# Row sums of a spatial gating weight moved from TensorE to VectorE, with a new place for the offsets and a new VectorE order

## What is computed

```
h = rms_norm(x); u, v, q, k, v2 = split(h @ w_in)
# spatial unit, blocks of 128 rows, 4 groups h of 128 channels
v = layer_norm(gelu(v), ln_g, ln_b)                  # ln_g, ln_b: one value per channel
w = where(mask, sgu_w, 0)                            # [4, 128, 128], upper right 64x64 corner is zero
mixed[p, c] = sum_q w[h][p, q] * v[q, c] + sgu_b[h, p]
y_a = gelu(u) * mixed
```

## Time and profile before

| | |
|---|---|
| median of 3 runs | 916.4 us |
| the profiled execution's own time | 916.97 us |
| its span in the trace | 915.2 us |
| TensorE busy | 906.9 us (99%) |
| VectorE, ScalarE, GpSimd busy | 593.3, 427.7, 394.2 us |
| granted TensorE clock | 0.999 of full speed |

### The profile page before, as it was taken

How to read it: one execution, slowest core, us unless ns; L and a number is a source line. 1 busy time by engine, 2 the same in 40 slices (tenths; PEclk the granted TensorE clock), 3 DMA queues, 4 the chain that set the end, 5 groups by cost and what they waited for, 6 DMA issues and landing times.

```text
span 915.2 us, 11923 instructions
## 1 busy us (share of the span) xinstructions
PE 906.9 (99%) x4209; PEld 747.4 (82%) x4209; DVE 593.3 (65%) x783; ACT 427.7 (47%) x832; POOL 394.2 (43%) x388
## 2 busy tenths in 40 slices
PE   9999999999999999999999999999999999999997
PEld 7888887787878888888888888888888888888885
DVE  6548989986679777475364653646557676544754
ACT  6637548857556533243333333333335455444451
POOL 1449743331243478567485675755754000000021
PEclk9999999999999999999999999999999999999999
DMA  9798465221343272743726437264367996556543
GB/s 338 229 270 253 105 171 137 70 88 51 110 121 105 81 229 75 225 149 116 230 82 218 148 117 230 84 216 148 117 211 255 355 392 200 196 191 199 185 138 138
DMA packets 152363, 159.58 MB, mean 174 GB/s; under 512 B 27752, under 2 KB 109680, under 8 KB 152304
## 3 DMA queue, kind: packets, MB, share of 16 engines
q1 hardware_dynamic: 151472, 157.89, 53.6%
q10 hardware_dynamic: 832, 0.92, 0.4%
HBM read 117.78 MB, written 40.50 MB: 173 GB/s over the span
## 4 chain that ended last, share of the span: by engine, by line
PE 83%; DVE 5%; DMA 3%; SPq 3%; issue 3%; POOL 2%; ACT 1%; POOLq 0%; DVEq 0%; ACTq 0%
PE ps L862 27%; PE ps L864 26%; PE ps L863 26%; DMA xs<-in_x 1%; SPq L387 1%; PE ps L1017 1%; PE ps L1042 1%; DVE wB_lo L1837 1%; PE ps L1029 1%; PE ps L1111 1%; DVE D_lo L1843 1%; DMA hT_raw<-in_xT 1%; POOL s L726 1%; DVE wA_lo L1837 1%; POOL by_offset L671 1%
## 5 line engine op out<-in xcount | busy, mean ns | idle before, releaser
L2096 DVE TENSOR_TENSOR P_lo<-P_raw,P_hi 128x512 fp32r<-128x512 f32 x132 | 124.2, 956 | 82.4 <-ACT P_hi L1536 76.7
L862 PE MATMUL ps<-T_hi,P_hi 128*128 128x512 f32 x352 | 136.9, 389 | 0.0
L863 PE MATMUL ps<-T_lo,P_hi 128*128 128x512 f32 x352 | 136.9, 389 | 0.0
L864 PE MATMUL ps<-T_hi,P_lo 128*128 128x512 f32 x352 | 136.9, 389 | 0.0
L804 POOL TENSOR_TENSOR wd<-wd 128x256 f32<-128x256 f32 x88 | 81.6, 928 | 93.4 <-DMA wd<-in_w_down 88.2
L862 PE MATMUL ps<-rb_hi,ra_hi 128*128 128x512 f32 x308 | 119.8, 389 | 0.0
L863 PE MATMUL ps<-rb_lo,ra_hi 128*128 128x512 f32 x308 | 119.8, 389 | 0.0
L864 PE MATMUL ps<-rb_hi,ra_lo 128*128 128x512 f32 x308 | 119.8, 389 | 0.0
L1650 ACT ACTIVATE ra_hi<-ra 128x512 fp32r<-128x512 f32 x77 | 48.6, 631 | 98.5 <-DMA rb<-w_down_T 59.8
L649 POOL TENSOR_SCALAR late<-late 128x1 f32<-128x1 f32 x12 | 6.1, 506 | 189.7 <-ACT junk L1718 176.2
L2205 DVE TENSOR_TENSOR ra_lo<-ra,ra_hi 128x512 fp32r<-128x512 f32 x77 | 55.8, 725 | 37.4 <-ACT ra_hi L1650 37.1
(11 more groups left out here) (281 smaller groups left out, 2012.7 us busy)
## 6 DMA issues: line engine op xcount, KB each, us to landing
wd<-in_w_down SPq DMA_DIRECT2D x44, 256.0 KB, 3.4
w_down_T<-wd SPq DMA_DIRECT2D x22, 512.0 KB, 4.7
ra<-act_S SPq DMA_DIRECT2D x44, 256.0 KB, 2.7
rb<-w_down_T SPq DMA_DIRECT2D x44, 256.0 KB, 3.0
act_S<-Q SPq DMA_DIRECT2D x33, 256.0 KB, 3.8
ra<-act_A SPq DMA_DIRECT2D x33, 256.0 KB, 4.6
rb<-in_w_down SPq DMA_DIRECT2D x33, 256.0 KB, 5.7
P_raw<-in_w_gate SPq DMA_DIRECT2D x22, 256.0 KB, 3.6
```

Of the source, the lines that this page charges most:

```text
L862: mm(dst, lhs[0], rhs[0], start=start, stop=False, skip_group_check=onto)
L863: mm(dst, lhs[0], rhs[1], start=False, stop=False, skip_group_check=onto)
L864: return mm(dst, lhs[1], rhs[0], start=False, stop=stop, skip_group_check=onto)
L2096: tt(w_l[p, m][:], src[:], w_h[p, m][:].bitcast(F32), ALU.subtract).then_inc(w_split, 1)
```

## The change

It takes the sums of w's rows on VectorE from the untransposed weights, which it loads as well, sends them through the same transpose and the same trip through DRAM as the row roots, and computes the offsets later. It also changes VectorE's order in four places (low parts of P4's weights, P5's second add, the woA pieces, the first softmax's list) and one place of ScalarE's.

```diff
--- before.py
+++ after.py
@@ -74,16 +74,14 @@
     wv_raw = [at(f"wv_raw{j}", 144 + 4 * j, [P, 2, C]) for j in range(4)]
     raw = [at(f"raw{s}", 160 + 4 * s, [P, D]) for s in range(2)]
     vn = at("vn", 144, [P, HA, T, P])
-    bsB = at("bsB", 188, [P, HA, P])
-    roots_all, root_rows = at("roots", 184, [P, 2, C]), at("root_rows", 206, [T, P])
+    bsB, sgu_rows = at("bsB", 182, [P, HA, P]), at("sgu_rows", 188, [P, HA, P])
+    roots_all, root_rows = at("roots", 184, [P, 2, C]), at("root_rows", 206, [T + HA, P])
     roots = [roots_all[:, h] for h in range(2)]
     kT, vT = at("kT", 192, [P, CH + ROWS]), at("vT", 196.25, [P, CH + ROWS])
     ident = at("ident", 200.5, [P, P])
     small = at("small", 201, [P, 256])
     sgu_wT, Bc = at("sgu_wT", 202, [P, HA, P]), at("Bc", 204, [P, HA, P])
     NV = K + 2 * HA
-    ones = at("ones", 206.5, [P, P], F32R)
-    sgu_hi, sgu_lo = at("sgu_hi", 176, [P, HA, P], F32R), at("sgu_lo", 178, [P, HA, P], F32R)
 
 
     PR = ("P1", "P2", "P6", "P5", "P7", "P3", "P4")
@@ -178,7 +176,8 @@
 
     gains = cols(NV)
     grp_g, ln_g, ln_b = gains[:, 0:K], gains[:, K:K + HA], gains[:, K + HA:NV]
-    ssq_x, ms_x, rstd_x = cols(T), cols(T), cols(T)
+    ssq_x, ms_x, root_cols = cols(T), cols(T), cols(T + HA)
+    rstd_x, sgu_sums = root_cols[:, 0:T], root_cols[:, T:T + HA]
     st_v, mv_v, ms_v, rstd_v = cols(6), cols(2 * T), cols(T), cols(T)
     ssqA, msA, rA = cols(T), cols(T), cols(T)
     ssqB, msB, rB = cols(T), cols(T), cols(T)
@@ -192,7 +191,7 @@
     ssq_h, ms_h = late[:, 6 * T:6 * T + HT], late[:, 6 * T + HT:7 * T]
 
     bias_dram = nc.dram_tensor("bias_by_offset", [CH, HB, KW], F32, kind="Internal")
-    root_dram = nc.dram_tensor("row_roots", [T, P], F32, kind="Internal")
+    root_dram = nc.dram_tensor("row_roots", [T + HA, P], F32, kind="Internal")
     x2_dram = nc.dram_tensor("x2_rows", [T, P, D], F32, kind="Internal")
     a_dram = {n: nc.dram_tensor(f"act_{n}", [IT, P, C], F32, kind="Internal") for n in ("A11", "A12", "A22", "S1", "S2", "S3", "S4")}
     wT_dram = nc.dram_tensor("w_down_T", [IT, 4, P, C], F32, kind="Internal")
@@ -234,8 +233,11 @@
     def in_at(p, i):
         return 4 + 4 * PR.index(p) + IN_ORDER[p].index(i) + 1
 
+    def in_high_at(p, i):
+        return 2 + 4 * PR.index(p) + i + 1
+
     def in_split_at(p, i):
-        return 2 + 4 * PR.index(p) + i + 1
+        return 2 + 4 * PR.index(p) + IN_ORDER[p].index(i) + 1
 
     def copied_at(p, i):
         return 4 * COPIED.index(p) + i + 1
@@ -406,6 +408,7 @@
             x_load(4)
             x_load(5)
             item_load(1)
+            sp.dma_start(sgu_rows[:], sgu_w.rearrange("h p q -> p h q")).then_inc(setup_in, 16)
             x_load(6)
             x_load(7)
             sp.wait_ge(x_sq, T)
@@ -420,7 +423,7 @@
                 sp.dma_start(xb[:, k, :], xT[1, k]).then_inc(block_in[k], 16)
             for k in range(4):
                 sp.dma_start(D_raw["D2"][:, k, :], xT[0, 4 + k]).then_inc(block_in[4 + k], 16)
-            sp.wait_ge(Bc_ready, 1)
+            sp.wait_ge(rowsum_done, 1)
             for t2 in range(2):
                 skew = bass.AP(tensor=bias_dram, offset=CH - 1 + t2 * KW, ap=[[HB * KW - 1, CH], [2 * KW, HB // 2], [1, WIN]])
                 sp.dma_start(bias[t2 * CH:(t2 + 1) * CH].rearrange("p g a j -> p (g a) j"), skew).then_inc(bias_in, 16)
@@ -662,7 +665,6 @@
                 nc.gpsimd.tensor_tensor(rstd_v[:, r:r + 1], ms_v[:, r:r + 1], minus_half[:, 0:1], ALU.pow).then_inc(v_rstd, 1)
 
             pool.wait_ge(consts_ready, 1)
-            nc.gpsimd.memset(ones[:].bitcast(F32), 1.0).then_inc(zero_ready, 1)
             nc.gpsimd.memset(kT[:, 0:CH], 0.0).then_inc(zero_ready, 1)
             nc.gpsimd.memset(vT[:, 0:CH], 0.0).then_inc(zero_ready, 1)
             pool.wait_ge(rel_in, 16)
@@ -895,15 +897,11 @@
                 gate_block(0, k)
             for k in range(K):
                 gate_block(1, k)
-                if k == 4:
-                    pe.wait_ge(wT_ready, 3)
-                    pe.wait_ge(zero_ready, 3)
-                    pe.wait_ge(v_ready, HT)
-                    mm(ps[:, 3, :], ones[:], sgu_hi[:].rearrange("q h p -> q (h p)"), start=True, stop=False)
-                    mm(ps[:, 3, :], ones[:], sgu_lo[:].rearrange("q h p -> q (h p)"), start=False, stop=True).then_inc(rowsum_done, 1)
                 if k == 5:
                     pe.wait_ge(x_rstd, 2)
-                    nc.tensor.transpose(ps[0:T, ROOT_BANK, 0:P], rstd_x, ident[:]).then_inc(rstd_T, 1)
+                    pe.wait_ge(rowsum_done, 1)
+                    pe.wait_ge(v_ready, HT)
+                    nc.tensor.transpose(ps[0:T + HA, ROOT_BANK, 0:P], root_cols, ident[:]).then_inc(rstd_T, 1)
 
             def unit(j):
                 c, half = UNITS[j]
@@ -1035,7 +1033,7 @@
                     pe.wait_ge(yb_totalled, r)
                 else:
                     pe.wait_ge(c_summed, added_at("P3", 3))
-                    pe.wait_ge(zero_ready, 4)
+                    pe.wait_ge(zero_ready, 3)
                     pe.wait_ge(vshift_in, 32)
                 for ci in range(2):
                     for g in range(KV):
@@ -1273,11 +1271,12 @@
             act_e.wait_ge(rel_built, 1)
             act_e.dma_start(bias_dram.ap()[:, :, 0:CH + WIN - 1], by_offset[:, :, 0:CH + WIN - 1]).then_inc(bias_out, 16)
             act_e.wait_ge(rstd_T, 1)
-            actv(root_rows[:], ps[0:T, ROOT_BANK, 0:P], ACT.Copy).then_inc(root_rows_ready, 1)
+            actv(root_rows[:], ps[0:T + HA, ROOT_BANK, 0:P], ACT.Copy).then_inc(root_rows_ready, 1)
             act_e.wait_ge(root_rows_ready, 1)
             act_e.dma_start(root_dram.ap(), root_rows[:]).then_inc(roots_out, 16)
             act_e.wait_ge(roots_out, 16)
-            act_e.dma_start(roots_all[:].rearrange("p h n -> p (h n)"), root_dram.ap().rearrange("t p -> (t p)").partition_broadcast(P)).then_inc(roots_in, 16)
+            act_e.dma_start(roots_all[:].rearrange("p h n -> p (h n)"), root_dram.ap()[0:T].rearrange("t p -> (t p)").partition_broadcast(P)).then_inc(roots_in, 16)
+            act_e.dma_start(Bc[:].rearrange("p h n -> p (h n)"), root_dram.ap()[T:T + HA].rearrange("t p -> (t p)").partition_broadcast(P)).then_inc(roots_in, 16)
             for r in range(HT, T):
                 gated_rows(r)
@@ -1360,7 +1359,7 @@
             def woA_piece(m):
                 act_e.wait_ge(raw_in[m % 2], 32 + 16 * (m // 2))
                 if m == 0:
-                    act_e.wait_ge(setup_in, 64)
+                    act_e.wait_ge(setup_in, 80)
                     act_e.wait_ge(prod_done, in_at("P6", 3))
                     act_e.wait_ge(d_summed, 16)
                 actv(woA_hi[:, m, :], raw[m % 2][:], ACT.Copy, scale=grp_g[:, m:m + 1]).then_inc(wo_hi_ready, 1)
@@ -1423,10 +1422,10 @@
             in_weight_hi("P4", 0)
             in_weight_hi("P4", 1)
             woA_piece(3)
+            in_weight_hi("P4", 2)
             ya_square(2)
             ya_hi_rows(2)
             ya_square(3)
-            in_weight_hi("P4", 2)
             ya_hi_rows(3)
             in_weight_hi("P4", 3)
@@ -1776,19 +1775,18 @@
                     dve.wait_ge(prod_done, in_at("P5", 3))
                 stt(woA_lo[:, m, :], raw[m % 2][:], grp_g[:, m:m + 1], woA_hi[:, m, :].bitcast(F32), ALU.mult, ALU.subtract).then_inc(wo_split, 1)
 
-            def setup_copies():
-                dve.wait_ge(setup_in, 64)
+            def row_sums():
+                dve.wait_ge(setup_in, 80)
                 nc.vector.memset(sgu_wT[CH:P, :, 0:CH], 0.0).then_inc(wT_ready, 1)
-                dve.wait_ge(wT_ready, 1)
-                copy(sgu_hi[:], sgu_wT[:]).then_inc(wT_ready, 1)
+                nc.vector.memset(sgu_rows[0:CH, :, CH:P], 0.0).then_inc(wT_ready, 1)
                 dve.wait_ge(wT_ready, 2)
-                tt(sgu_lo[:], sgu_wT[:], sgu_hi[:].bitcast(F32), ALU.subtract).then_inc(wT_ready, 1)
+                nc.vector.tensor_reduce(sgu_sums, sgu_rows[:], AX.X, ALU.add).then_inc(rowsum_done, 1)
 
             def offsets():
-                dve.wait_ge(rowsum_done, 1)
-                dve.wait_ge(setup_in, 64)
+                dve.wait_ge(roots_in, 32)
+                dve.wait_ge(setup_in, 80)
                 for h in range(HA):
-                    last = stt(Bc[:, h, :], ps[:, 3, h * P:(h + 1) * P], ln_b[:, h:h + 1], bsB[:, h, :], ALU.mult, ALU.add)
+                    last = stt(Bc[:, h, :], Bc[:, h, :], ln_b[:, h:h + 1], bsB[:, h, :], ALU.mult, ALU.add)
                 last.then_inc(Bc_ready, 1)
                 for ci in range(2):
                     for t2 in range(2):
@@ -1804,7 +1802,6 @@
                 wv_block(k)
                 xT_lo(0, k)
             xT_lo(1, 0)
-            setup_copies()
             for k in range(1, K):
                 xT_lo(1, k)
             for r in range(HT):
@@ -1814,7 +1811,7 @@
             v_centre(HT - 1)
             item("k")
             item("v")
-            offsets()
+            row_sums()
```

(27 more changed lines are left out.)

## The result

The changed kernel takes 922.88 us (median of 6 runs, 922.36 to 925.04) against 916.4 us before: ratio 1.0076, 95% interval 1.0066 to 1.0086. It is slower by 6.5 us; 919.2 was forecast. The profiled execution took 922.95 us with a span of 921.1.

A forecast was written before the change was run, and what follows sets the result against it. TensorE bounds the kernel, busy 906.9 of 915.2 us. Terms -0.03 + 3.6 + 0.2 - 0.15 - 0.75 - 0.17 + 0.1 = +2.8 us on the 916.4 median gave 919.2 us; 8-in-10 range 915.4 to 920.8.

The forecast's parts named there:

- The offsets in their new place: Ahead of the first spatial product: four offsets each wait a GpSimd turn, ending at 80.0 us; TensorE idles 3.2 us.
- The term of 0.4 for the later chain: Row-sum weight load of 256 KB queues ahead of D1's and D2's blocks, delaying the chain to D2 by 0.4 us.
- The clock: Rival: idling ahead of the first spatial product drops TensorE to 1.2 GHz, 2 to 3.5 us more, 922 us; chance 0.06.
- The other order changes: VectorE's reordered list around the first softmax: minus 0.15, 0.75 and 0.17 us, plus 0.1 given back.
- 0.1 given back: At the transpose of the sum of squares at 172.5 us, which has little slack: plus 0.1 us (0 to 0.4).
- The three old waits: TensorE waits inside P5, ahead of the first logits and ahead of P4: 0.15, 0.75 and 0.17 us to be won.
- The rule about two SBUF inputs: VectorE instructions reading two SBUF tensors alternate with GpSimd, one whole instruction each; 1.30 us a turn for the offsets.
- The first eviction covered: Second broadcast load delays ACT and the first eviction by under 0.4 us; TensorE needs it some 4 us later: 0.
- The root as cover for the row sums: The transpose waits for POOL's root, ending at 43.95 us: row sums cost 0, the matmuls' 0.45 us gain shrinks to 0.03.
- The sinks: Four instructions behind the offsets: 0.69 us, at worst 5.2 in turns; rival with turns, 923.7 us, chance 0.04.

The follow-up runs named there:

- sinks_away: The changed kernel with the four small sink instructions moved behind the row sums at 42 us, offsets left in place; 921.18 us, ratio 1.0052.
- pool_yields: The changed kernel with GpSimd's first sum of P5's and P7's weight blocks held until the offsets are done; 921.1 us, ratio 1.0053.
- filled_wait: The changed kernel with 15 matmuls of 128x512 into an unused bank ahead of the first spatial product; 924.6 us, ratio 1.0092.
- sums_only: The changed kernel with only row sums and offsets changed, all VectorE and ScalarE orders as in the kernel before; 921.25 us, ratio 1.0056.
- order_only: The kernel before with the new orders alone, row sums still on TensorE and offsets at 42 us; 917.71 us, ratio 1.0015.
- order_swap: order_only with low parts of ya's rows 2 and 3 ahead of `normal_probs(0)` and woA's last piece behind `corner(P4, 3)`; 916.12 us, ratio 1.0002.
- eight_offsets: The changed kernel with each of the four offset instructions of 128 elements cut into two of 64; 928.09 us, ratio 1.0123.
- early_swap: offsets_early with low parts of ya's rows 2 and 3 ahead of `normal_probs(0)` and woA's last piece behind `corner(P4, 3)`; 918.3 us, ratio 1.0032.
- offsets_early: The changed kernel with the offsets directly behind `evict(2)`, at about 66.5 us, where GpSimd stands idle; 918.04 us, ratio 1.0029.
- sums_clean: sums_only with offsets behind `evict(2)`, sinks at 42 us and `evict(3)` ahead of the second low part of D2; 916.9 us, ratio 1.0006.

## Why the prediction was wrong

The direction and the main mechanism were right, the size was not: +2.8 forecast, +6.5 measured, outside the range. Two steps failed. The sum had nothing for the slower matmuls behind the wait (1.8 us measured), and it followed the new list only as far as the softmax and priced what lies behind it at 0.1 (1.8 measured). Another 0.5 us of the miss is in no step: the sum was read from an execution of the kernel before that lay 0.6 above its median.

*The offsets in their new place: right.* Four turns of 1.30 us to 80.0 were forecast; they took 5.22 us and ended at 80.20. Excess at the first spatial product 3.4 against 3.6. The term of 0.4 for the later chain: the low part ended at 75.06 instead of 74.83, 0.2.

*The clock: the largest single miss.* It stood as a rival with a chance of 0.06 and a price of 2 to 3.5 us; with the 1.8 us that it cost here the sum would have come to 4.6. The waits of 3.25 us (changed), 3.08 (sinks_away), 3.28 (pool_yields) and 2.79 (filled_wait) were all followed by a mean granted clock of 0.60 to 0.68 over four microseconds. The Trainium skill (TensorE: Matmul & The Clock Gate, Part 1) has idleness halve the clock; these four traces agree, the two waits of sums_only (2.86 and 2.74 us) did not bring it down.

*"The other order changes", the sentence that ended with 0.1 given back: wrong.* The three old waits went nearly as computed (1.07 us; 0.09 is left at the logits). But the path behind `normal_probs(0)` was followed to the transposes only, and the low parts of ya, which the list had moved beside GpSimd's gates, were costed as if alone. The rule about two SBUF inputs, used for the offsets, was not applied to them. They cost 1.2 us in C and 0.6 in D; order_only and order_swap show this as the list's own doing.

*The first eviction covered, the last one overlooked.* `evict(3)` stands behind two low parts of D2. TensorE was 0.44 earlier, the eviction 0.24 later, and P1's second unit waited 0.37 us.

*The root as cover for the row sums: right in kind, not in this execution.* The transpose started at 43.67, since the root ended at 43.42 instead of 43.95, so all of the 0.45 us was kept. In pool_yields and eight_offsets it did wait for the root, 0.6 and 0.3 us.

*The sinks: the bound of 5.2 us was right (4.94), its chance of 0.04 wrong.* The row beside a GpSimd operation of 128x4 said nothing of one beside 128x512. What it costs depends on when TensorE needs `ya_mix(0)`: here it ended at 89.30 us for a product due at 89.30, and 0.15 was lost; in sums_only it ended at 89.52 for one due at 86.77, in pool_yields at 87.67 for 84.38, in filled_wait at 90.54 for 87.73, and TensorE waited some 3 us. `spatial(2)` is due 7.24 us behind the start of `spatial(0)` (84.15 in the kernel before), not 7.5.

Summed again with what was measured: -0.44 + 0.37 + 3.4 + 1.8 + 0.15 - 1.07 + 1.2 + 0.6 = +6.0, the difference of the spans. The sum hits that closer than its terms do: by the marks, A grew by 3.44 where the first three terms give 3.33, and C shrank by 0.03 where they give +0.13.

## What to carry to other kernels

Count instructions, not elements, when VectorE works with two SBUF inputs beside a GpSimd that streams: each waits for one whole operation of the other, so short instructions belong where GpSimd stands idle, or should read PSUM. Go through every instruction that a reordering moves and ask what GpSimd does at its new time. A wait on TensorE of some 3 us can bring slower matmuls behind it, here half as much again; give that a real chance in the sum.

## What the runs showed of the hardware

Two engines in strict turns: 1.31 us for 64 elements, 1.35 for 128, 1.77 for 512 (the qT of the earlier trace rows), each beside GpSimd's sums of 128x512, against 0.34 for 128 elements alone. What was not expected is that a `tensor_scalar` of 64x4 float32 with a single SBUF input takes turns as well: 1.24 instead of 0.17 us. The Trainium skill (SBUF — State Buffer, section SBUF: two separate sides) lists, besides two SBUF inputs, VectorE's 2-port modes as needing the shared pair; the traces don't name the mode of this instruction, but they agree in that it waits.

Not expected either: the granted clock fell behind waits of 2.79 to 3.28 us (and in or behind those of 3.76 and 7.90) and stayed full behind the 2.86 and 2.74 us of sums_only. Since it fell behind 2.79 and not behind 2.86, the length of the wait alone doesn't decide; what does was not found. And a start of GpSimd that differed by 0.6 us (67.20 in early_swap, 67.82 in offsets_early, whose lists are the same up to there) decided over whole turns, which fits the scatter of several us in both kernels' runs.

That order_swap and sums_clean, with spans of 914.3 and 914.1 us in their profiles, are no faster than the kernel before in the median has a plain reason for the greater part: the 915.2 of the kernel before belongs to an execution 0.6 above its median (its executions beside later runs had spans from 913.8 to 915.4), and the 914.1 of sums_clean to one 1.0 below its own. How long its old waits are in those was not traced.
